# A decoder block with routed experts: sigmoid's table load, the table of visits, one added product, and slots turned one pair ahead

## The reference

```python
def moe(u, router_w, router_b, w_gate, w_up, w_down):
    scores = jax.nn.sigmoid(xt.astype(jnp.float32) @ router_w.astype(jnp.float32))
    sel = scores + router_b.astype(jnp.float32)
    ...                                    # best group of 4 experts, its top 2: top_idx
    weights = top_s / jnp.sum(top_s, axis=-1, keepdims=True)
    combine = jnp.sum(jax.nn.one_hot(top_idx, N_EXPERTS, dtype=jnp.float32) * weights[..., None], axis=1)
    for e in range(N_EXPERTS):             # 16 experts
        he = jax.nn.silu(xt @ w_gate[e]) * (xt @ w_up[e])       # 1024 -> 512
        out = out + combine[:, e:e + 1] * (he @ w_down[e])      # 512 -> 1024
```

## Time and profile before

| | us |
|---|---|
| median of 3 runs | 605.34 (604.6 to 606.64) |
| profiled execution, its time | 606.29 |
| its span, first to last instruction | 604.5 |
| mean granted PE clock, as a share of full speed | 0.989 |
| PE busy | 581.9 (96%) |
| DVE busy | 307.1 (51%) |
| ACT busy | 238.9 (40%) |

### The profile page before, as it was taken

One profiled execution on the slowest core, in us unless ns is written; L12 is line 12 of the kernel. 1 busy time (PEld: TensorE's weight loads), 2 busy tenths in 40 slices (PEclk: granted clock), 3 DMA queues, 4 the chain that ended last, 5 costly groups with the idle time before them and its releaser, 6 DMA issues.

```text
span 604.5 us, 8460 instructions
## 1 busy us (share of the span) xinstructions
PE 581.9 (96%) x3561; PEld 425.9 (70%) x3561; DVE 307.1 (51%) x461; ACT 238.9 (40%) x330; POOL 9.0 (1%) x23
## 2 busy tenths in 40 slices
PE   3999999999999999999999999899999999999995
PEld 1789988999998888999999988533533443353332
DVE  0679976766568876687455682602121130212204
ACT  4626647444455455674672334711111020111113
POOL 3010000000000000000000000000000000000000
PEclk9998999999999999999999999899999999999998
DMA  8999554785858946726659989299999999999991
GB/s 312 387 341 313 199 200 140 279 294 214 295 210 310 367 155 243 269 80 210 209 209 357 401 326 371 110 366 423 420 423 420 420 423 421 420 422 421 421 352 71
DMA packets 51578, 184.78 MB, mean 306 GB/s; under 512 B 3650, under 2 KB 3762, under 8 KB 37714
## 3 DMA queue, kind: packets, MB, share of 16 engines
q1 hardware_dynamic: 50706, 183.53, 78.8%
q10 hardware_dynamic: 704, 0.58, 0.3%
q0 software_dynamic: 128, 0.11, 0.1%
HBM read 183.16 MB, written 1.05 MB: 305 GB/s over the span
## 4 chain that ended last, share of the span: by engine, by line
PE 92%; ACT 3%; DVE 2%; DMA 1%; issue 1%; SPq 0%; ACTq 0%; DVEq 0%
PE ps L1571 30%; PE ps L1781 18%; PE ps L1593 15%; PE ps L1793 8%; PE ps L1827 3%; PE ps L1769 2%; DMA first_ada<-in_ada_w_dram 1%; PE ps L1552 1%; PE ps L1803 1%; PE ps L1657 1%; PE ps L1693 1%; PE ps L1678 1%; PE ps L1489 1%; PE ps L1820 1%; PE ps L1582 1%
## 5 line engine op out<-in xcount | busy, mean ns | idle before, releaser
L952 DVE TENSOR_TENSOR lo<-raw,hi 128x2048 fp32r<-128x2048 f32 (+1 forms) x51 | 114.2, 2248 | 42.1 <-ACT hi L612 41.8
L1571 PE MATMUL ps<-u_hi,hi 128*128 128x256 f32 x416 | 120.0, 288 | 0.4 <-DVE lo L952 0.4
L1571 PE MATMUL ps<-u_lo,hi 128*128 128x256 f32 x416 | 117.7, 283 | 0.0
L1571 PE MATMUL ps<-u_hi,lo 128*128 128x256 f32 x416 | 117.7, 283 | 0.0
L1781 PE MATMUL ps<-ring,xe_t 128*64 128x512 f32 x512 | 113.3, 594 | 0.0
L612 ACT CAST hi<-raw 128x2048 fp32r<-128x2048 f32 x50 | 94.8, 1908 | 37.2 <-PE ps L1571 26.3
L1781 PEld LDWEIGHTS ps<-ring,xe_t 128*64 128x64 f32 x512 | 35.9, 137 | 67.8 <-issue 67.4
L1571 PEld LDWEIGHTS ps<-u_hi,hi 128*128 128x128 f32 x416 | 79.7, 192 | 1.6 <-issue 0.8
L1571 PEld LDWEIGHTS ps<-u_lo,hi 128*128 128x128 f32 x416 | 79.7, 192 | 0.2
L1571 PEld LDWEIGHTS ps<-u_hi,lo 128*128 128x128 f32 x416 | 79.7, 192 | 0.0
L1793 PE MATMUL ps<-ring,he_t 128*64 128x512 f32 x224 | 49.6, 595 | 0.0
(11 more groups left out here) (332 smaller groups left out, 846.0 us busy)
## 6 DMA issues: line engine op xcount, KB each, us to landing
raw<-in_w_in_dram SPq DMA_DIRECT2D x41, 1024.0 KB, 5.4
ring<-in_w_gate_e_dram SPq DMA_DIRECT2D x32, 1024.0 KB, 17.2
ring<-in_w_up_e_dram SPq DMA_DIRECT2D x32, 1024.0 KB, 16.1
ring<-in_w_down_e_dram SPq DMA_DIRECT2D x28, 1024.0 KB, 16.0
raw<-in_ada_w_dram SPq DMA_DIRECT2D x16, 1024.0 KB, 5.3
first_ada<-in_ada_w_dram SPq DMA_DIRECT2D x16, 512.0 KB, 11.8
raw<-in_w_branch_m_dram SPq DMA_DIRECT2D x4, 1024.0 KB, 6.5
raw<-in_w_out_dram SPq DMA_DIRECT2D x4, 1024.0 KB, 5.6
```

Of the source, the lines that this page charges most:

```text
L952: ins = V.tensor_tensor(lo[b % RING][:, tiles, :], src[:, tiles, :], hi[b % RING][:, tiles, :].bitcast(F32), ALU.subtract)
L1571: ins = mm(dst, w[:, k, cols], x[:, k0 + k, :], start=(first and c % 2 == 0 and k == 0 and n == 0), stop=(end and k == KB - 1 and n == 2), ...
```

## The change

Four edits:

- ACT waits for `logits_all1` alone before the sigmoid, no longer for `logits_all0` too (the second event of one engine implies the first).
- L1343 signals an event of its own, `most`; PE's second gather waits for it in place of `ranks`, and the first low rows of tile 1 are made ahead of `slot_tab`, not behind it.
- One product of the identity with 256 columns of mod[0] into bank ps3 stands behind the first `start_sums`; its result is not used.
- In the loop `turn_slots` of pair p + 1 stands in pair p, between `turn_he` and the second `scatter`, and `take_slots` of p + 1 behind `weigh` of p. Pair 0's own stay where they were. There are three `scat` buffers (the new one lies where `rw_scaled` was) and three columns in `w_slot`. Down of pair p now waits for `scat_ready` of p + 2, so for the next pair's `take_slots`, since both use ps7. The wait for `y_out` before `turn_slots` is gone.

```diff
         shift_part = at("shift_part", tables_at + 1344 / K + 512 / K, [P, KT, NE])
+        scat.append(at("scat2", tables_at + 1344 / K, [P, T], F32R))
...
-        w_slot = small("w_slot", [P, 2])
+        w_slot = small("w_slot", [P, 3])
...
             x1_root(1)
-            after(act, "logits_all0", "logits_all1")
+            after(act, "logits_all1")
             event(A_(rt[:, 0], rt[:, 1], ACT.Sigmoid), "scores")
...
-            V.tensor_reduce(many[:, 0:1], ps[5][:, TT * NE:(TT + 1) * NE], AX_X, ALU.max)
+            event(V.tensor_reduce(many[:, 0:1], ps[5][:, TT * NE:(TT + 1) * NE], AX_X, ALU.max), "most")
+            low_rows(1, 0).then_inc(xg_split, 1)
             for t in range(TT):
                 ins = V.tensor_tensor(slot_tab[:, t, 0:VISITS * NE].rearrange("p (v e) -> p v e", e=NE),
                                       rt[:, R, t, :].unsqueeze(1).broadcast_to([P, VISITS, NE]), slot_off[:], ALU.add)
             event(ins, "ranks")
-            low_rows(1, 0).then_inc(xg_split, 1)
...
-                dve.wait_ge(slots_turned, p + 1)
-                take_slots(p % 2)
+                if p == 0:
+                    dve.wait_ge(slots_turned, 1)
+                    take_slots(0)
                 if p % 2 and p < PAIRS - 1:
                     build_onehot(p // 2 + 1)
                 dve.wait_ge(scat_ready, p + 1)
                 dve.wait_ge(sg_ready, p + 1)
                 dve.wait_ge(chunk_used, 2 * (p * NPART + 4))
-                weigh(p % 2)
+                weigh(p % 3)
+                if p < PAIRS - 1:
+                    dve.wait_ge(slots_turned, p + 2)
+                    take_slots((p + 1) % 3)
...
             start_sums(0, 0)
+            for _ in range(1):
+                mm(ps[3][:, 0:T], ident[:], mod[:, 0, 0:T], start=True, stop=True)
             after(pe, "picked")
...
-            after(pe, "ranks")
+            after(pe, "most")
             gather_part(1, 4 * SLOTS, 5, (0,))
...
-                pe.wait_ge(y_out, 2 * p)
                 if p == 0:
                     pe.wait_ge(weights_split, 1)
-                turn_slots(col, weights[:, :, 2 * p:2 * p + 2])
+                    turn_slots(0, weights[:, :, 0:2])
...
-                    scatter((p - 1) % 2, 0)
+                    scatter((p - 1) % 3, 0)
...
                 turn_he()
+                if p < PAIRS - 1:
+                    if p == 0:
+                        pe.wait_ge(scat_ready, 1)
+                    if p % 2:
+                        pe.wait_ge(onehot_ready, p // 2 + 2)
+                    turn_slots((p + 1) % 2 * 2 * SLOTS, weights[:, :, 2 * p + 2:2 * p + 4])
                 if p:
-                    scatter((p - 1) % 2, 1)
+                    scatter((p - 1) % 3, 1)
...
-                pe.wait_ge(scat_ready, p + 1)
+                pe.wait_ge(scat_ready, min(p + 2, PAIRS))
                 pe.wait_ge(he_t_ready, p + 1)
```

More of the change, by code:

```diff
@@ L366, in plan @@
             dve += ["x1_1_t0", "x1_var0", "x1_rms0", "x1_1_t1_0", "x1_1_t1_1", "logits_all0", "x1_copied1_t1", "x1_var1", "x1_rms1",
-                    "logits_all1", "picked", "rank0", "ranks", "comb", "many"]
+                    "logits_all1", "picked", "rank0", "most", "ranks", "comb", "many"]
         plan()
```

## The result

The median of six runs is 602.22 us (600.97 to 602.85) against 605.68 us for six runs of the kernel before (604.6 to 606.64): 3.5 us less, ratio 0.994 with a 95% interval of 0.9926 to 0.9954. The forecast was 601.2 us. The profiled execution has a span of 599.1 us where before it was 604.5.

What follows compares the result with a forecast made beforehand. The matrix engine (PE) was taken to bound the kernel, 92% of the last chain. Router 2.26 us (load 1.16, clock 0.9, order 0.2) plus loop 1.9 made 4.16 us, from 605.34 to 601.2 us, range 599.8 to 603.3.

Steps and rivals of the forecast that it cites:

- The table load: Router: ACT's load before the sigmoid starts earlier, at 376.69 us, so scores and all behind them come 1.16 us earlier.
- The clock: Router: PE's clock stays at 1.00 through the gathers where it fell to 0.50; worth 0.9 us.
- The rival that the clock falls anyway: Router: the clock still drops, so the router brings only 1.16 us; 602.3 us, chance 0.12.
- the slower rival: Loop, between up and down: the clock falls for 3.25 us, costing 1.6 us a pair; 612.6 us, chance 0.03.
- The product costs nothing: Router: the added product, about 0.43 us, fits PE's idle time before the rank products as long as "picked" comes later.
- The table of visits: Router: slot_tab behind the second low rows lets the low gathers start about 0.2 us earlier.
- The turn: Loop: moving turn_slots saves 0.67 us between gate and up, costs 0.40 behind turn_he; net 0.27 a pair, 1.9 in all.
- The new wait: Loop: down waits for the next pair's take_slots, which is ready with 0.1 us of room.
- the rival in which the turn takes its full price: Loop: turn costs 0.50 us plus 0.1 to 0.2 of wait, so the loop brings nothing; 603.1 us, chance 0.12.
- the transfers: Last pair: PE could catch up with the weight transfers; 3.0 us of room, 1.1 left; as a rival 602.3 us, chance 0.05.
- the first and third rival: Router's clock falls anyway, chance 0.12; PE runs into the transfers in the last pair, chance 0.05; each 602.3 us.
- the rest: Router: the load does not move and the product alone keeps the clock up; 602.3 us, chance 0.02.

Runs made afterwards that it cites:

- sigmoid_only: The kernel before with only the sigmoid's wait for logits_all0 removed; 602.99 us against 605.36, ratio 0.9968.
- no_product: The changed kernel without the added product; 602.65 us against 605.99 for the kernel before, ratio 0.995.
- slots_only: The kernel before with only the loop's edits, slots turned a pair ahead; 603.99 us against 605.99, ratio 0.9974.
- turn_before_he: The changed kernel with turn_slots moved ahead of turn_he, behind the first scatter; 600.84 us, measured again 601.81; ratios to the kernel before 0.9927 and 0.9942.
- three_products: The changed kernel with three added products in place of one; 601.55 us in one run, 605.37 for the kernel before.
- router_only: The kernel before with only the three router edits (sigmoid's wait, added product, low rows ahead of slot_tab); 602.68 us against 605.99, ratio 0.995.
- after_again: The changed kernel, nothing altered, measured a second time; 601.29 us against 605.37 for the kernel before, ratio 0.993.

## Why the prediction was right, and where it was off

The direction and the range held: 602.22 us in 599.8 to 603.3. The forecast said 4.16 us less, 3.46 were measured and 3.56 stand in the traces. Of the 1.0 us between 601.2 and 602.22, 0.70 is this gain and 0.34 the base: six runs of the kernel before have a median of 605.68, the three known then 605.34. That the second measurement, 601.29, all but meets the forecast is luck, since two medians of one kernel lie 0.9 us apart.

- **The table load: right.** 1.16 us forecast, 1.15 seen, by itself in `sigmoid_only`. The load starts as soon as ACT is free (374.86 us, L818 ended at 374.84), and the sigmoid stands 0.02 us behind its end, as forecast.
- **The clock: right in the place and size, wrong in who did it.** 0.9 us forecast, 0.82 seen. The prediction had it with the added product, which cuts the idle time to 0.4 us, but `sigmoid_only` and `no_product` have it without. The cause that the runs show is the idle time that the load's move takes away, from 1.99 to 0.85 us. The argument "from 376 to 377 it stopped for 0.44 us and the clock held" was weak: in `slots_only` the clock fell behind those very stops. The rival that the clock falls anyway may have more to it than the profiled executions show, as the timed runs of `no_product` and `turn_before_he` with a mean clock of 0.985 to 0.990 suggest. A reading was off too: by the earlier trace rows the clock came back at 386.3 and not at 386.15, so the fall lasted 3.4 us and not 3.25. The sum does not use it; only the slower rival's price does, which becomes 1.7 us for 1.6.
- **The product costs nothing: right.** PE was idle for 0.42 us with it and 0.85 without it. `three_products` shows a little more room than that: 1.28 us of product made the rank products 0.28 us late, so 1.0 us was free.
- **The table of visits: right.** 0.2 us forecast, 0.28 seen.
- **Behind the low gathers: a term was missing.** 0.16 us of the 2.25 are lost there (218.30 for 218.14 in `router_only`). 0.09 of it is in the first low gathers, which take 1.05 us to the next piece (382.27 to 383.32) and took 0.96. They start 0.06 us behind the end of their low rows, so PE may have stopped for these, but no trace shows such a wait. The rest is no more than the 0.07 us by which the two traces of the changed kernel differ (216.83 and 216.90).
- **The turn: the mechanism right, both terms of the sum mis-sized.** "0.67 us less" at the old place measured 0.64, and "I take 0.40" at the new one measured 0.42 to 0.44: the turn itself 0.36 (0.14 and 0.22), and `turn_he` 0.08 more with it behind. So a pair gains 0.20 to 0.22 and not 0.27, and the loop, seven times that, 1.47 us and not 1.9. Together with the lost 0.16 that is the 0.6 us by which 4.16 was too much.
- **The new wait: right.** `take_slots` ends 0.24 us before down starts, where 0.1 was forecast, since down starts 1.44 us behind the turn's first record and `take_slots` ends 1.20 behind it, for 1.4 and 1.25; the rival in which the turn takes its full price did not come. Nor did the transfers (1.5 us of room where 1.1 was forecast), nor a fall of the clock in the loop, where it is 1.00 from 392 to 590 us in every profiled execution.
- **The chances: one sum does not fit its words.** The forecast, the first and third rival and the rest make 0.85, so that 0.90 for "under 603.5" takes in 0.05 of the second rival's 0.12, which is not most of it.

## What to carry to other kernels

A wait for two events of one engine, where the later implies the earlier, need not be free if a table load stands behind it: here the load took a wait with it and could not go ahead. Where a short stop of PE is followed by a lower clock, look first for what makes the stop long, and count both; here one deleted wait gave 1.15 us of chain and 0.82 us of clock. A piece with another tile shape between two like blocks cost more here than its own records, 0.64 us for 0.48 (448.93 to 449.41 in the earlier trace rows): take it out and put it beside pieces of its own shape, and count what remains of it there, two thirds in this case.

## What the runs showed of the hardware

The clock does not fall at the same places in each execution of the same code. Ahead of the change, over 44 to 52 us it was 0.79 in some profiled executions (before, `no_product`, `after_again`) and 1.00 in the others, over 312 to 340 us 0.94 or 1.00, and in `slots_only` it fell in the last logits while in before it held there. The scaling of the last logits starts at 377.35 to 377.54 us in the three executions with both falls and at 375.61 to 376.18 in the six with neither. The changed kernel has one of each: 375.70 in its first trace, 377.35 in the second. The distance, up to 1.9 us, is half of what the whole change brings, so a comparison of two single spans would have said 5.4 us for 3.5.
